# A hybrid layer's first norm: turning and splitting x without its token factor, and multiplying the factor in where products leave their banks

## The reference, cut to what matters

```python
def rms_norm(x, g):
    xf = x.astype(jnp.float32)
    xf = xf * lax.rsqrt(jnp.mean(xf * xf, axis=-1, keepdims=True) + NORM_EPS)
    return (xf * g.astype(jnp.float32)).astype(x.dtype)

def hybrid_layer(x, positions, norm_mix, w_in, b_gate, ...):
    h = rms_norm(x, norm_mix)
    proj = h @ w_in          # 21 groups of columns: queries, keys, values, gates of four mixers
    ...
    gates = jax.nn.sigmoid((gate_logits + b_gate).astype(jnp.float32))
    mixed = jnp.sum(gates.reshape(B, S, N_BRANCH, D_MODEL) * branch, axis=2)
    x = x + mixed @ w_out
    h2 = rms_norm(x, norm_ff)
    return x + jnp.square(jax.nn.relu(h2 @ w_ff1)) @ w_ff2
```

## Time and profile before

| | |
|---|---|
| time, median of 3 runs | 1714.39 us (1713.72 to 1714.65) |
| span of the profiled execution | 1712.5 us, first to last instruction; no other time of that execution is given |
| TensorE busy | 1655.2 us, 97% |
| VectorE, ScalarE, GpSimd busy | 911.1, 733.2, 139.0 us |
| mean granted TensorE clock | 0.994 of full speed |
| first transpose of layer 0, of layer 1 | 614.38 us, 1160.30 us |

### The profile page before, as it was taken

How to read it: one execution, slowest core, us unless ns; L and a number is a source line. 1 busy time by engine, 2 the same in 40 slices (tenths; PEclk the granted TensorE clock), 3 DMA queues, 4 the chain that set the end, 5 groups by cost and what they waited for, 6 DMA issues and landing times.

```text
span 1712.5 us, 23478 instructions
## 1 busy us (share of the span) xinstructions
PE 1655.2 (97%) x9575; PEld 1239.2 (72%) x9575; DVE 911.1 (53%) x1547; ACT 733.2 (43%) x1111; POOL 139.0 (8%) x133
## 2 busy tenths in 40 slices
PE   7999999988988989999999999999999999999998
PEld 6986434443444369888788888888978878888886
DVE  6584211111112065755588877536665557978744
ACT  5663111111111145655556365334755554645532
POOL 0000000000000001323200000000323210000000
PEclk9999999999999999999999999999999999999999
DMA  7457999999999956434454445536443445445552
GB/s 310 156 210 320 384 422 427 428 429 429 429 429 425 417 218 247 172 112 160 150 213 171 163 189 197 206 147 234 192 157 145 161 162 182 183 162 197 197 205 87
DMA packets 39184, 420.49 MB, mean 246 GB/s; under 512 B 4048, under 2 KB 5680, under 8 KB 12336
## 3 DMA queue, kind: packets, MB, share of 16 engines
q1 hardware_dynamic: 39088, 419.12, 62.0%
HBM read 417.24 MB, written 1.87 MB: 245 GB/s over the span
## 4 chain that ended last, share of the span: by engine, by line
PE 88%; DMA 9%; DVE 1%; ACT 1%; issue 1%; SPq 0%; POOL 0%; POOLq 0%; DVEq 0%; ACTq 0%
PE bank L1313 10%; DMA work_mem<-in_w 7%; PE bank L1989 7%; PE bank L1535 6%; PE bank L1533 5%; PE bank L1534 5%; PE bank L1559 5%; PE bank L1560 5%; PE bank L1565 5%; PE bank L1998 4%; PE bank L1338 3%; PE bank L1486 3%; PE bank L1493 3%; PE bank L1487 3%; DMA wring<-in_w 2%; PE bank L1034 1%
## 5 line engine op out<-in xcount | busy, mean ns | idle before, releaser
L3132 DVE TENSOR_TENSOR w_lo<-wring,w_hi 128x2048 fp32r<-128x2048 f32 x84 | 192.1, 2290 | 110.3 <-ACT w_hi L2310 110.3
L2310 ACT ACTIVATE w_hi_early<-wring 128x2048 fp32r<-128x2048 f32 x84 | 161.0, 1917 | 205.2 <-PE bank L1565 120.7
L2310 ACT ACTIVATE w_hi<-wring 128x2048 fp32r<-128x2048 f32 x84 | 161.0, 1917 | 193.6 <-PE bank L1534 88.2
L3132 DVE TENSOR_TENSOR w_lo<-wring,w_hi_early 128x2048 fp32r<-128x2048 f32 x84 | 203.7, 2427 | 44.7 <-ACT w_hi_early L2310 44.5
L1313 PE MATMUL bank<-wring,gates_mem 128*64 128x512 f32 x720 | 162.9, 595 | 7.8 <-DMA wring<-in_w 7.8
L1559 PE MATMUL bank<-w_hi_early,mixed 128*128 128x512 f32 x384 | 151.7, 395 | 0.0
L3029 DVE TENSOR_TENSOR gates_mem<-bank,gates_mem 128x512 f32<-128x512 f32 x32 | 22.1, 692 | 241.9 <-ACT gates_mem L2254 126.8
L1560 PE MATMUL bank<-w_hi_early,mixed 128*128 128x512 f32 x384 | 149.7, 390 | 0.0
L1989 PE MATMUL bank<-mixed,w_hi 128*128 128x512 f32 x512 | 123.0, 391 | 0.0
L1313 PEld LDWEIGHTS bank<-wring,gates_mem 128*64 128x64 f32 x720 | 52.9, 137 | 96.8 <-issue 95.6
L1989 PEld LDWEIGHTS bank<-mixed,w_hi 128*128 128x128 f32 x512 | 93.9, 188 | 18.1
(11 more groups left out here) (534 smaller groups left out, 3093.4 us busy)
## 6 DMA issues: line engine op xcount, KB each, us to landing
wring<-in_w SPq DMA_DIRECT2D x157, 2048.0 KB, 8.7
work_mem<-in_w SPq DMA_DIRECT2D x32, 2048.0 KB, 17.1
gates_mem<-rel_skew SPq DMA_DIRECT2D x16, 512.0 KB, 9.1
work_mem<-in_w SPq DMA_DIRECT2D x2, 1024.0 KB, 14.3
work_mem<-in_w SPq DMA_DIRECT2D x4, 512.0 KB, 18.4
cst<-in_const SPq DMA_DIRECT2D x1, 1224.0 KB, 15.7
prm<-in_prm SPq DMA_DIRECT2D x3, 381.0 KB, 8.9
x_mem<-in_x SPq DMA_DIRECT2D x2, 512.0 KB, 4.4
```

What stands on the lines that cost most here:

```text
L2310: act.activation(hi, w, ACT.Copy).then_inc(hi_ready, 1)
L3132: dve.tensor_tensor(lo, w, hi, ALU.subtract).then_inc(lo_ready, 1)
```

## The change

x is turned as it is, without the factor of the token; gains still go in when the turned x is rounded. The factor, one number for each token, is spread over all partitions by two matmuls (a new job, factor) into token_factor, and multiplied in where products leave their banks: VectorE does this for products with features on partitions (by_token, 15 a layer, copies that ScalarE made before, but without a factor), ScalarE by its scale for products with tokens on partitions, and the gate rows' addition takes it as well. For layer 0 the final norm's gain and the layer's gain become one vector, first_gain, made in the first block.

The transposes move to turn_first and turn_all: at layer 0 they follow the adds, at layer 1 three quarters of them stand ahead of the last group of ff2 matmuls. The first three products are made by first_fill, in another order of passes. At layer 0 GpSimd rounds the first half chunk, and at both layers it makes its low part. Half of the turned x is rounded by VectorE. Squares, variance and power stay, but later in each engine's order. Chunk 0 is loaded in two halves of columns (pieces of 1 KB), and the gain row after it. nsa_q[1] moves ahead of rope_k and hid_cmp(0), both rope_q behind nsa_v; the two window sums share a bank, and so do kc and vc. SP's order of chunks and its table of uses stay.

The diff, cut to its core:

```diff
@@ plan_layer @@
-    for name, count in (("ht", 4), ("nsa_k", 3), ("dup", 2), ("nsa_q", 1), ("rope_k", 1), ("hid", 1), ("nsa_q", 1), ("rope_q", 1),
-                        ("nsa_v", 1), ("rope_q", 1), ("narrow", 1), ("hid", 1), ("nsa_f", 1)):
+    for name, count in (("ht", 4), ("nsa_k", 3), ("factor", 1), ("nsa_q", 1), ("dup", 2), ("nsa_q", 1), ("rope_k", 1), ("hid", 1),
+                        ("nsa_v", 1), ("rope_q", 2), ("narrow", 1), ("hid", 1), ("nsa_f", 1)):
@@ SP @@
-        sp.dma_start(gain_row, d["gain"][0]).then_inc(gain_loaded, 16)
...
+                if c == 0:
+                    for half in range(2):
+                        cols = slice(half * 256, half * 256 + 256)
+                        source = d["w2"][LAYER_SOURCE[c] + l * LAYER_CHUNKS].rearrange("p (k n) -> p k n", k=KT)
+                        sp.dma_start(view(layer_slot(c), 0, KT, 512)[:, :, cols], source[:, :, cols]).then_inc(
+                            w_landed[c % RING] if half else first_half_landed, 16)
+                    if l == 0:
+                        sp.dma_start(gain_row, d["gain"][0]).then_inc(gain_loaded, 16)
@@ TensorE @@
+        def turn_first(l, i, half):
+
+            n = 2 * i + half if l == 0 else 2 * half + i
+            added, at = (moe["spread", 0][n], last_turn) if l == 0 else (layer["ff2"][n], l - 1)
+            pe.wait_ge(bank_read[added.bank], added.count(at))
+            for n, j in enumerate(layer["ht"][2 * half:2 * half + 2]):
+                if i == 0:
+                    free(j, l)
+                for t in range(2):
+                    dt = 4 * half + 2 * n + t
+                    mm = pe.transpose(psum[j.bank][:, t * S + i * P:t * S + (i + 1) * P], x[:, i, dt * P:(dt + 1) * P], ident)
...
+            def first_fill(two, third):
...
+                pe.wait_ge(first_high, TT + l + 1)
+                for j in two:
+                    free(j, l)
+                high_pass(range(4))
+                if l:
+                    turn_first(l, 1, 1)
+                    high_half(1)
+                    free(third, l)
+                    third_pass(third_hi, h_hi, range(4), True)
+                    high_pass(range(4, KT))
+                else:
+                    high_pass(range(4, KT))
+                    high_half(1)
+                    free(third, l)
+                    third_pass(third_hi, h_hi, range(4), True)
+                third_pass(third_hi, h_hi, range(4, KT))
+                pe.wait_ge(first_low, 2 * TT + l + 1)
...
-            split_first(layer["nsa_k"][:2])
-            split_a(layer["nsa_k"][2], high_half(1), 0, h_parts, True, low=1)
+            first_fill(layer["nsa_k"][:2], layer["nsa_k"][2])
+            pe.wait_ge(params2_loaded, 16 * l + 16)
+            j = layer["factor"][0]
+            free(j, l)
+            pe.wait_ge(in_rstd_ready, TT * l + TT)
+            for i in range(TT):
+                mm = pe.matmul(psum[j.bank][:, i * P:(i + 1) * P], in_rstd[:, i:i + 1].to_broadcast([P, P]), ident, start=True,
+                               stop=True)
+            mm.then_inc(bank_full[j.bank], 1)
+            split_a(layer["nsa_q"][0], high_half(2), 0, h_parts, True, low=2)
             for n in range(2):
                 dup_cmp(n)
-            split_a(layer["nsa_q"][0], high_half(2), 0, h_parts, True, low=2)
+            split_a(layer["nsa_q"][1], high_half(3), 0, h_parts, True, low=3)
             rope_of("rope_k", 0, [k_sw[:, t, :] for t in range(2)])
             hid_cmp(0)
-            split_a(layer["nsa_q"][1], high_half(3), 0, h_parts, True, low=3)
-            rope_of("rope_q", 0, [q_n[:, t, :] for t in range(2)])
             split_tokens(layer["nsa_v"][0], half_ready(4), 0, S)
-            rope_of("rope_q", 1, [q_n[:, 2 + t, :] for t in range(2)])
+            for n in range(2):
+                rope_of("rope_q", n, [q_n[:, 2 * n + t, :] for t in range(2)])
@@ TensorE, end of a layer @@
             for n in FF2_LAST:
+                if n == FF2_LAST[-1] and l < LAYERS - 1:
+                    for i, half in ((0, 0), (0, 1), (1, 0)):
+                        turn_first(l + 1, i, half)
@@ ScalarE @@
             if l == 0:
                 used = moe["down", 0][-1]
                 act.wait_ge(bank_full[used.bank], used.count(last_turn))
+            else:
                 split_hi(0)
+            split_hi(1)
+            act.wait_ge(params2_loaded, 16 * l + 16)
+            if l == 0:
+                act.wait_ge(first_gain_ready, 4 + 1)
+            high_x(layer["ht"][0:2], at2["norm_mix"] if l else first_gain)
@@ GpSimd @@
         for l in range(LAYERS):
+            c, w, hi, lo = weight_half(0)
+            if l == 0:
+                used = moe["down", 0][-1]
+                pool.wait_ge(bank_full[used.bank], used.count(last_turn))
+                pool.wait_ge(first_half_landed, 48 + 16)
+                pool.tensor_copy(hi, w).then_inc(first_high, 1)
+            pool.wait_ge(first_high, TT + l + 1)
+            pool.tensor_tensor(lo, w, hi, ALU.subtract).then_inc(first_low, 1)
             rsqrt_in(l, in_var, in_rstd)
@@ VectorE @@
+            def by_token(j, out, scale=1.0):
+
+                full(j, l)
+                tiles = out.shape[1]
+                dve.scalar_tensor_tensor(out, psum[j.bank][:, 0:tiles * S].rearrange("p (a n) -> p a n", a=tiles), scale,
+                                         token_factor.rearrange("p (o n) -> p o n", o=1).to_broadcast([P, tiles, S]),
+                                         ALU.mult, ALU.mult).then_inc(bank_read[j.bank], 1)
...
+            dve.wait_ge(first_low, 2 * TT + l + 1)
+            split_lo(1)
+            if l == 0:
+                dve.wait_ge(gain_loaded, 16)
+                for half in range(2):
+                    for i in range(TT):
+                        gain_x(i, half)
+                split_lo(2)
+                first_factors()
...
+                if name in FEATURE_MAJOR:
+                    by_token(layer[name][n], FEATURE_MAJOR[name][:, 2 * n:2 * n + 2, :], HD ** -0.5 if name[-1] == "q" else 1.0)
+                elif name == "gla_qk":
+                    by_token(layer[name][n], (q_g, k_g)[n], (GLA_DK ** -0.5, 1.0)[n])
```

More of the change, by code:

```diff
@@ L2338, in fill @@
                 next_hi(filler_half[name, n])
-                j = layer[name][n]
-                pair = slice(2 * n, 2 * n + 2)
                 if name == "gates":
@@ L2382, in _ @@
             act.activation(bias_rows[0:4 * KT, :], psum[layer["nsa_f"][0].bank][0:4 * KT, P:2 * P], ACT.Copy)
-            copy(layer["nsa_f"][0], flat(fg), turn=l, cols=64)
+            for i in range(TT):
+                ins = act.activation(fg[:, i, :], psum[layer["nsa_f"][0].bank][:, 32 * i:32 * i + 32], ACT.Copy,
+                                     scale=in_rstd[:, i:i + 1])
+            ins.then_inc(bank_read[layer["nsa_f"][0].bank], 1)
             def compress(kind, n):
-                j = layer[kind][n]
+                if (kind, n) == ("hsum", 0):
+                    return
+                j = layer["kc"][0] if kind == "vc" else layer[kind][0 if kind == "hsum" else n]
@@ L3047, in gain_x @@
         def gain_x(i, half):
-            j, cols = moe["spread", 0][2 * i + half], slice(half * 512, (half + 1) * 512)
-            dve.wait_ge(bank_read[j.bank], j.count(last_turn))
+            cols = slice(half * 512, (half + 1) * 512)
             dve.tensor_tensor(xg[:, i, cols], x[:, i, cols], gain_row[:, cols], ALU.mult).then_inc(xg_ready, 1)
@@ L3102, in _ @@
             dve.memset(mark, 0.0).then_inc(moe_done, 1)
-            for half in range(2):
-                for i in range(TT):
-                    gain_x(i, half)
         with dve.Else():
@@ new lines, in _ @@
+            dve.wait_ge(params2_loaded, 16 * l + 16)
+            if l == 0:
+                dve.wait_ge(first_gain_ready, 4 + 1)
+            gain = at2["norm_mix"] if l else first_gain
+            for n, j in enumerate(layer["ht"][2:4]):
+                full(j, l)
+                for t in range(2):
+                    dt = 4 + 2 * n + t
+                    ins = dve.tensor_scalar(h_hi[:, dt, :], psum[j.bank][:, t * S:(t + 1) * S], gain[:, dt:dt + 1], None, ALU.mult)
+                ins.then_inc(hT_hi_ready, 1)
@@ new lines, in _ @@
+            low_x(layer["ht"][0:2], gain, h_lo, 0)
+            for n, j in enumerate(layer["ht"][2:4]):
+                dve.wait_ge(hT_hi_ready, 2 + 2 * l + n + 1)
+                for t in range(2):
+                    dt = 4 + 2 * n + t
+                    ins = dve.scalar_tensor_tensor(h_lo[:, dt, :], psum[j.bank][:, t * S:(t + 1) * S], gain[:, dt:dt + 1],
+                                                   h_hi[:, dt, :], ALU.mult, ALU.subtract)
+                ins.then_inc(bank_read[j.bank], 1)
@@ L3153, in _ @@
+            j = layer["factor"][0]
+            full(j, l)
+            dve.tensor_copy(token_factor, psum[j.bank][:, 0:S]).then_inc(bank_read[j.bank], 1)
+            dve.wait_ge(bank_read[j.bank], j.count(l))
```

(5 more changed lines are left out.)

281 lines of the change are left out of this document (145 added, 136 removed).

## The result

The changed kernel takes 1724.38 us (median of 4 runs, 1722.30 to 1724.81); the kernel before took 1714.52 beside it. The ratio is 1.0054, 95% interval 1.0042 to 1.0066: 9.9 us slower where 3.5 us faster was forecast, and outside the range. The profiled execution has a span of 1720.5 us, against 1712.5.

The account below looks back on a forecast made before the run. TensorE, busy 97% of the span, was taken as the bound, with gains only at the two layer starts. 3.05 us in layer 0 plus 0.5 in layer 1 gave 3.5 off 1714.39: 1710.9 us, range 1705.5 to 1715.3.

Parts of the forecast that it names:

- TensorE starts the products at 610.9: Layer 0: first products start once the first turned pair is rounded; they end at 622.9, 7.9 us earlier than before.
- signs of being wrong: Products of layer 0 after 613, GpSimd subtraction much over 5 us, TensorE waiting for VectorE-read banks, clock 0.50 after 652.
- the clock falls in the new waits: Rival, chance 0.24: half clock after the waits of hid_cmp(1), 1.7 us a fall; 1712.6 for one, 1714.3 for two.
- the checkpoint: TensorE reaching hid_cmp(1), from where work order is as before: 657.40 and 1203.59 before, 654.35 and 1203.1 forecast.
- The factor's wait: Layer 0, after the first three products: TensorE idles some 2 us from 622.9 until squares, variance and power are done.
- The wall: Chunks 5 and 4 go out together after hid_cmp(0), take 12.95 us; hid_cmp(1) waits 2.5 us for chunk 4.
- Layer 1: Products end at 1173.7 against 1177.00, mostly eaten by the wall; hid_cmp(1) at 1203.1, 0.5 us earlier.
- GpSimd's part: Layer 0, first half chunk: rounding 2.2 us and low part 4.4 us, hidden with 3 us to spare.
- Copies on VectorE: 15 products a layer copied by VectorE instead of ScalarE, 0.75 us each, 11 us a layer; cost taken as 0.
- The change doesn't do what it says: Rival: TensorE's stall at 608.94 stays near 5 us, ScalarE awaiting the second half; 1714; chance 0.13 shared with late start.
- The chances: Forecast 0.38, faster in 6 of 10; clock falls 0.24, in 1 of 4; no wall 0.14, always; total written 0.45.

Follow-up runs that it names:

- a_no_branch: The changed kernel with TensorE's If taken out, so no jump between the last transposes and the first products: 1717.08 us, ratio 1.0014.
- b_no_branch: The kernel before the change with TensorE's If taken out in the same way: 1714.38 us, ratio 0.9999.
- a_arms_swapped: The changed kernel with TensorE's two arms in the other order, so the jump stands at the entry: 1722.56 us, ratio 1.0044.
- a_act_rounds: The changed kernel with layer 0's rounding of the first half chunk given back from GpSimd to ScalarE: 1723.83 us, ratio 1.0057.
- fill_arms_mid: Changed kernel with chunk 4 loaded before chunk 5, narrow's copies first, layer 0's first products in both arms, factor inside first query product: 1707.86 us, 0.9961.

## Why the prediction was wrong, point by point

- **The step that failed: "TensorE starts the products at 610.9".** It came from the operands alone. They would have let TensorE start at about 611.3 (the last transpose ended at 610.51, and a_no_branch waits 0.75 us there). It started at 616.11, 5.2 us later than forecast, and 4.8 of these because it had just jumped out of an arm. Neither the sum nor a rival had a price for that. The row was in sight: the 5.45 us of the earlier trace rows were put down wholly to VectorE, as the profile names it. That was true as far as it went (b_no_branch), but a wait shows the last cause only, and the one beneath was not asked for. Two of the prediction's own signs of being wrong then stood in the profile: products after 613, and the clock at 0.50 after 652.
- **The rival "the clock falls in the new waits" came true**, on top of that, and three times in layer 0: behind the two new waits, and behind the old stall, which the forecast had taken away. Products 13.45 us (616.11 to 629.56, the factor row's start less its wait) in place of 12.0: 1.45 (a_no_branch, at full clock: 12.17). From the factor to the end of hid_cmp(0), 17.6 in place of 16.2: 1.4. And hid_cmp(1) itself: 1.55 (behind the checkpoint, so not in the sum below). Each fall cost 1.4 to 1.55 us where the rival took 1.7. Which wait is followed by a fall was left open, rightly: behind 3.27 us in a_arms_swapped hid_cmp(1) ran at full clock (1.96), behind 2.24 in a_no_branch at half (3.56).
- **The factor's wait** was 3.03 us and not 2; with the matmuls behind it 3.5 us against 2.3 in the sum, 1.2 more. It is the same 3.03 in a_no_branch, so it is not the late products that made it: the term was mis-sized of itself. From ScalarE's start on half 2 (626.06) to the factor's matmuls it is 6.53 us in place of 5.75, with two powers of 0.55 one after the other where one was counted; and ScalarE starts on half 2 3.50 us before the products end where 3.7 was counted.
- **The wall** was read rightly: both chunks go out behind hid_cmp(0) (SP at 650.80), waits of 3.27 and 2.32 us against 2.5 forecast. In layer 0 the stretch from hid_cmp(0)'s end is 13.88 us in place of 12.95: 0.9, and why the two chunks took that much longer stays open. That the wall could be undone by a swap of two numbers was not said.
- In layer 0 these terms make 5.2 + 1.45 + 1.2 + 1.4 + 0.9 = 10.15 us: hid_cmp(1) was forecast at 654.35 and came at 664.54, 10.2 later.
- **Layer 1** came as forecast in this one execution: 0.58 us earlier, 0.5 forecast. It has no jump.
- **GpSimd's part**: 1.89 and 4.57 us; hidden, as said, and worth nothing as long as the jump stands (a_act_rounds). The 4497 ns that the prediction takes from the Trainium skill, GPSIMD Engine Reference, section 3.1, stand there for an addition of this size; the subtraction measured 4.57 us.
- **Copies on VectorE**: taken as 0, rightly. TensorE has no wait for VectorE between 670 and 1155, and from hid_cmp(1) of layer 1 to the end it is 508.75 us against 508.91.
- **"The change doesn't do what it says"** was half right in the number (a stall of 5.6 stays) and wrong in its cause (ScalarE waiting for the second half), and in its time: 1714 supposed that nothing else is lost.
- Of the 9.9 us between the medians the two profiled spans show 8.0. The profiled execution of the changed kernel is the fastest of its four: its span is 1720.5, those of the others 1722.5 to 1723.0, at a mean granted clock of 0.991 or 0.992 in place of 0.993. Each run's time is 1.8 us above its own span. So some 2 us of a usual run, at a lower clock, are not in the profile read here, and where they arise stays open.
- The chances: 0.38 x 0.6 + 0.24 / 4 + 0.14 makes 0.43 for a faster kernel, where 0.45 was written. It changes nothing here.

## What to carry to other kernels

A wait has a last cause, and may have others just as long beneath it. Before taking its work away, ask what else the engine does in it, above all whether its own program jumps there; an "issue" wait, or a packet on the instruction queue inside a wait, is the sign. If a long arm must be jumped over, end it where the engine waits anyway and where the DMA queues are quiet. And when the order of jobs changes, the order of loads that was written for the old one has to change with it: here that was 6.8 us between the medians, for two numbers.

## What the runs showed of the hardware

A jump over one experts' turn or more left TensorE idle for 4.93 to 5.91 us at the arm's exit with the loads flowing (426 GB/s in the change), for 3.02 with next to none, and for 1.77 behind the 96 first products, with next to none. At the arm's entry it was 3.22 and 2.75 us, with 401 to 451 GB/s flowing. A jump over a few instructions cost nothing that the trace shows. With each of the long jumps one packet of 16 KB is found on the queue of code, and none there in the runs without one. From that packet to the next matmul it was 2.7 to 2.9 us, with loads and without, and 2.5 in fill_arms_mid. What this part consists of is not explained. The packet was found 2.2 to 3.1 us behind the last matmul at the exit with loads flowing, 0.1 behind it without, and at most 0.4 behind it at the entry; for the entry the reason was not settled.
